# Expert slots handled in pairs, and the last token half's input projection dealt out among its attention units

## The chip, the cores and the metric

The kernel runs as one program on one core of a Trainium2 chip. The metric is the device time of one execution, in microseconds. TensorE is called PE below, VectorE DVE, ScalarE ACT, GpSimd POOL and SyncE SP.

## What is computed

Two transformer blocks follow each other on 512 tokens of width 1024, all in float32.

The first block ends with a mixture of tiny experts (PEER). For each token and each of 8 heads, 16 experts are chosen out of 16,384. Each chosen expert has a row `u` and a row `v` of 1024 numbers:

```python
pre = jnp.einsum('cd,chkd->chk', hc, u[ec])
coef = gc * jax.nn.gelu(pre, approximate=False)
out = jnp.einsum('chk,chkd->cd', coef, v[ec])
```

The second block puts 16 learned tokens ahead of the 512, normalizes, and projects to queries, keys, values (8 heads of 64), 8 forget gates and 512 pooling channels. Queries and keys are normalized per head. Then it computes

```python
s = einsum("bhqd,bhkd->bhqk", q, k) * scale + (cum_logf_q - cum_logf_k)   # causal, then softmax
p = softmax(s);  a_out = einsum("bhqk,bhkd->bhqd", p, v)
pooled[g] = trailing_mean(u[g], window 2, 4, 8 or 16) - u[g];  p_out = (pooled @ w_pool) * pool_scale
h = h + concat(a_out, p_out) @ w_out
h = h + (silu(n2 @ w_gate) * (n2 @ w_up)) @ w_down
```

The first block's attention, gates and projections come before all of this and are not touched by the change.

## The kernel before, in words

**Expert slots.** Four tiles of 128 tokens times 8 heads times 16 experts make 512 slots, numbered n. For each slot POOL issues one indirect DMA (`gather`, L1560) that fetches for 128 tokens a row of 8 KB, u and v together, about 1.05 MB. There are 8 buffers (`SLOT = 8`); a buffer is refilled when PE has used it (`rows_used`). Then DVE multiplies with the token and sums (`dots(n)`, L1585), ACT applies Gelu, multiplies with the router weight and writes a diagonal matrix (`diagonal(n)`: L1299, L1303, L1309), and PE adds the weighted v rows into PSUM (`combine(n)`, L850). `combine` is called at even n only and takes slots n and n+1 together, 8 matrix products on 64 x 64 quarters of the array. ACT and DVE handle one slot in each turn of their loops. Between the slots DVE chooses the experts of later heads (`choose`, cut into parts by `PLAN`), with one exponential on ACT (`best_weights`, L1264).

**The second block in two halves.** `block2(g)` is written once for each engine as a Python generator and works on a pair of token tiles, 256 tokens: g = 0 with the 16 learned tokens ahead (272 columns), then g = 1. The generators count ticks; `ticks.until(t)` yields until tick t, and the fixed numbers `T_IN`, `T_A`, `T_O` and so on say at which tick a step stands. For g = 0 the generators run inside the slot loops: after the work of slot n each engine advances its generator by `ticks_at(n)`, which is 0 up to slot 275 and from there 1, and 2 at every fourth slot (5 ticks in 4 slots). For g = 1 the generators run after the last slot, with nothing between the ticks. Each engine executes its own program in order; engines wait for each other by semaphores only.

**Order inside one half.** Two norms; 12 tiles of the input projection (4 of queries, 4 of keys, 4 of pooling channels; `in`, L925, 8 products each), with for each of the 8 query and key tiles a product that sums squares (`square`, L921), a logarithm and an exponential on ACT (`root`, L1334 and L1336) and a scaling on DVE; the forget gates (L931); the values (L945); the trailing means on DVE and four pooling products (L956). Only then come the 16 attention units, two per head, u = 0 to 15, one per 128 tokens. In the half g = 1 unit u works on 400 (u even) or 528 (u odd) keys:

- PE `scores(u)`: three products each, q times k with 64 rows (L972), the cumulated gates with 8 rows (L973), the causal mask (L975). 528 columns don't fit one bank, so odd units do it for 16 and for 512 columns.
- DVE takes the maximum (L1953), ACT the exponential with its sum (L1416), DVE the reciprocal (L1959), ACT scales (L1427).
- PE `transposes(u)` (L986, L988, L990), ACT copies them out of PSUM (L1440 to L1443), PE `values(u)` (L1004, L1006).
- On PE the order is scores(u), values(u-3), transposes(u-1); ACT and DVE handle unit u three ticks after PE's scores(u).

After the units come the output projection (L1028), which waits for all parts of `mix`, a norm, gate and up projections (L1046) and the down projection (L1059).

**Weights** come through SP's queue in a fixed order into a ring of 4 slots of 512 KB, each refilled when PE has finished the tile that was in it (`tile_done`). PSUM banks are handed out ahead of time by `bank_claims`, in program order.

Of the kernel before, what the change touches and what calls it, by code (L numbers as in the profile page):

```python
# [57 lines left out]
T_IN, T_FG, T_V, T_POOLED, T_P, T_A, T_O, T_U, T_D, T_END = 20, 44, 46, 47, 59, 62, 120, 146, 234, 285  # L58
ROTATE = [(0, 1, 2, 3), tuple(range(8))]
# [16 lines left out]
def ticks_at(n):  # L76

    return 0 if n < FIRST_TICK else 1 + (n % 4 == 0)

# [5 lines left out]
def bank_claims():  # L85

    table, count, sums = {}, [0] * 8, [0] * 8
    for g in range(2):
# [15 lines left out]
        for m in range(12):  # L104
            next_bank("in", m)
            if 3 <= m < 11:
                next_bank("square", m - 3)
        next_bank("forget")
        for b in range(3 - g):
            next_bank("v", b)  # L110
        for b in range(2):
            next_bank("pool", b)
# [82 lines left out]
def program(nc, xT, metaT, cond, w_ada, small, onehot, rel_bias, w_stream, sub_keys, experts, outT):  # L195
# [5 lines left out]
    with ctx:  # L201
# [116 lines left out]
        h_tok = take(TT, D)  # L318
        rows = take(SLOT, 2 * D)
# [33 lines left out]
        pooled = mix[:, 0:4, :]  # L353
# [18 lines left out]
        pool_a, pool_b = prob  # L372
# [16 lines left out]
        def wait_full(eng, g, *name):  # L389

            if name[0] in BY_TILE:
# [9 lines left out]
        def bank_of(g, *name):  # L401
            return CLAIMS[(g, *name)][0][0]
# [125 lines left out]
        def _(sp_eng):  # L528
# [35 lines left out]
            for n in range(FIRST_BLOCK // SLOTS * SLOTS, RING_TILES):  # L564
# [4 lines left out]
                eng.wait_ge(tile_done.sem, tile_done.ready(n - SLOTS))  # L569
                eng.dma_start(ring[:, n % SLOTS, :], w_stream[n if n < FIRST_BLOCK else FIRST_BLOCK + t])\  # L570
# [8 lines left out]
        def _(pe):  # L579
# [290 lines left out]
            def block2(g):  # L870
# [40 lines left out]
                for m in range(12):  # L911
# [16 lines left out]
                yield from ticks.until(T_FG)  # L928
                b = taken("forget")
                for k in range(KT):  # L930
                    last = mm(bank(b, wide)[0:NH, :], vec[:, B_FG + k * NH:B_FG + (k + 1) * NH], n_t[:, k, 0:wide],  # L931
                              start=k == 0, stop=k == KT - 1)
                last.then_inc(bank_full[b], 1)

                for t in range(4):
                    for c in range(3 - g):
# [13 lines left out]
                yield from ticks.until(T_P)  # L950
                w = stationary(B_POOL)
                for c in range(4):
                    if c % 2 == 0:
                        b = taken("pool", c // 2)
                    pe.wait_ge(pooled_ready.sem, pooled_ready.ready(g * 4 + c))
                    last = mm(bank(b, PAIR, c % 2 * PAIR), w[:, c, :], pooled[:, c, :], start=True, stop=True)  # L956
                last.then_inc(tile_done.sem, 1)

                def scores(u):
# [4 lines left out]
                    if u % 4 == 0:  # L964
                        pe.wait_ge(qk2_ready.sem, qk2_ready.ready(g * 8 + 4 + u // 4))
# [43 lines left out]
                for u in range(19):  # L1009
# [55 lines left out]
            for n in range(HEADS * PK):  # L1065
# [12 lines left out]
                for _ in range(ticks_at(n)):  # L1078
                    next(pair, None)
# [9 lines left out]
        def _(act):  # L1089
# [206 lines left out]
            def diagonal(n):  # L1296
                s = n % SLOT
                act.wait_ge(pre_done.sem, pre_done.ready(n))
                steps(op(pre[:, s:s + 1], pre[:, s:s + 1], ACT.Gelu))  # L1299
# [3 lines left out]
                steps(op(coef[:, s:s + 1], pre[:, s:s + 1], ACT.Copy, scale=wgt[:, n // P % 2, n % P:n % P + 1]))  # L1303
                if n >= SLOT:
                    act.wait_ge(rows_used.sem, rows_used.free(n, SLOT))
# [3 lines left out]
                op(diag[:, s, :], ident_pair, ACT.Copy, scale=coef[:, s:s + 1]).then_inc(diag_done.sem, 1)  # L1309
# [7 lines left out]
            def block2(g):  # L1317
# [39 lines left out]
                for m in range(12):  # L1357
                    if m < 12:
                        yield from ticks.until(T_IN + 2 * m + 4)
                        b = full("in", m)  # L1360
                        if m == 0 and g == 0:
                            act.wait_ge(chosen.sem, chosen.ready(3 * PH - 1))
                        dst = (q2[:, m % 4, 0:wide], k2[:, m % 4, cols], u2[:, m % 4, cols])[m // 4]
                        ins = op(dst, bank(b, wide), ACT.Copy)
                        ins.then_inc(in_ready.sem, 1)
                        if m < 8:
                            if m >= 3:
                                full("square", m - 3)
                            steps(op(square2[:, m % 3, 0:wide], bank(b, wide), ACT.Square))
                            steps.wait()  # L1370
                            act.sem_inc(square2_ready.sem, 1)
                        act.wait_ge(in_ready.sem, in_ready.ready(g * 12 + m))
                        act.sem_inc(bank_free[b], 1)
                    if 3 <= m < 11:
                        if m >= 5:
                            act.wait_ge(root2_used.sem, root2_used.ready(g * 8 + m - 5))
                        root((m - 3) % 2, wide, "square", m - 3)

                yield from ticks.until(T_FG + 4)
                act.wait_ge(forget_ready.sem, forget_ready.ready(g))  # L1380
                if g == 0:
                    act.preload_act_table_set("natural_log_exp_and_others")
                steps(op(logs[0:NH, 0:wide], logs[0:NH, 0:wide], ACT.Exp, scale=-1.0))
                steps.wait()
                op(logs[0:NH, 0:wide], logs[0:NH, 0:wide], ACT.Ln, bias=1.0).then_inc(forget_log.sem, 1)

                for c in range(3 - g):
                    yield from ticks.until(T_V + 12 + c)
# [10 lines left out]
                for c in range(4):  # L1399
                    yield from ticks.until(T_P + 3 + c // 2)  # L1400
# [4 lines left out]
                    else:  # L1405
# [3 lines left out]
                        act.sem_inc(bank_free[b], 1)  # L1409

# [39 lines left out]
                for u in range(19):  # L1450
# [3 lines left out]
                    if u % 4 == 2 and u > 2:  # L1454
                        b = full("y", u // 4 - 1)
                        steps(op(mix[:, u // 4 - 1, :], bank(b, PAIR), ACT.Copy))
                        steps.wait()
                        act.sem_inc(mix_ready.sem, 1)
                        act.sem_inc(bank_free[b], 1)
# [26 lines left out]
            for n in range(HEADS * PK):  # L1486
                h, c = n // PK, n % PK
                diagonal(n)
# [14 lines left out]
                for _ in range(ticks_at(n)):  # L1503
                    next(pair, None)
# [63 lines left out]
        def _(dve):  # L1568
# [296 lines left out]
            def block2(g):  # L1865
# [31 lines left out]
                for m in range(8):  # L1897
                    yield from ticks.until(T_IN + 2 * m + 12)
                    roots(2 + m)
                    dve.wait_ge(in_ready.sem, in_ready.ready(g * 12 + m))  # L1900
                    a = q2[:, m, 0:wide] if m < 4 else k2[:, m - 4, cols]
                    gain = col[:, 12:13] if m < 4 else vec[:, QN + 1:QN + 2]
                    steps(stt(a, a, gain, root2[m % 2][:, 0:wide], ALU.mult, ALU.mult))
# [4 lines left out]
                yield from ticks.until(T_FG + 3)  # L1908
                b = full("forget")
                steps(V.tensor_scalar(forget[0:NH, 0:wide], bank(b, wide)[0:NH, :], vec[0:NH, BF:BF + 1], None, ALU.add))  # L1910
                tell(dve, steps, bank_free[b])
                steps(stt(logs[0:NH, 0:wide], forget[0:NH, 0:wide], -1.0, forget[0:NH, 0:wide], ALU.mult, ALU.max))
                tell(dve, steps, forget_ready)

                n = 0
                for c in range(4):
# [4 lines left out]
                    for a in range(c + 1):  # L1921
                        yield from ticks.until(T_POOLED + n // 2)
                        n += 1
                        dst = (pool_a, pool_b)[a % 2]
# [5 lines left out]
                    yield from ticks.until(T_POOLED + n // 2)  # L1930
                    n += 1
                    steps(stt(pooled[:, c, :], src[:, META:META + PAIR], 1.0 / (2 << c), u[:, META:], ALU.mult, ALU.subtract))
                    tell(dve, steps, pooled_ready)
                    if c == 1:
                        dve.wait_ge(forget_log.sem, forget_log.ready(g))
                        steps(stt(forget[0:NH, 0:wide], forget[0:NH, 0:wide], 0.0, logs[0:NH, 0:wide], ALU.min, ALU.subtract))
                        steps.wait()
                        steps(V.tensor_tensor_scan(cum[0:NH, cols], ones[0:NH, 0:1].to_broadcast([NH, wide]),
                                                   forget[0:NH, 0:wide], 0.0, ALU.mult, ALU.add))
                        steps.wait()  # L1940
# [152 lines left out]
```

## Time and profile before

| | |
|---|---|
| median of 3 runs | 2644.8 us (2644.13 to 2647.96) |
| the profiled execution | 2649.4 us, its span 2647.6 us |
| mean granted PE clock | 0.89 |
| busy: PE, DVE, ACT, POOL | 2197.7, 1327.1, 1036.6, 581.2 us |
| expert rows by the indirect DMAs | 540.07 MB in 512 gathers |
| expert slots | from about 690 to 2166 us |
| half g = 1 of the second block | from about 2176 us to the end |

Busy time is given per engine; a PE that is busy is not PE at its full clock. The granted clock is 1.00 at 2.4 GHz and 0.50 at 1.2 GHz.

### The profile page before, as it was taken

The page shows a single profiled execution, that of the slowest core. Times are in us where ns is not written, and L with a number is a line of the kernel's source. Part 1 is how long each engine was busy: PE and PEld are TensorE (multiplying, and loading weights), DVE is VectorE, ACT ScalarE, POOL GpSimd, SP SyncE. Part 2 cuts the span into 40 slices and gives each one's busy share as a digit, 9 for nine tenths or more (in the row PEclk, how much of TensorE's full clock was granted, in tenths as well). Part 3 has the DMA queues.
Part 4 walks back from the last instruction along what each step waited for, and adds up shares of the span by engine and source line. Part 5 has one row for each costly group of instructions (what it writes and reads, how often), then busy time and mean ns, then how long its engine had stood idle before and what let it go on. Part 6 is the DMA issues. An engine that isn't in the chain of part 4 may idle for free.

```text
span 2647.6 us, 30679 instructions
## 1 busy us (share of the span) xinstructions
PE 2197.7 (83%) x10876; PEld 1328.3 (50%) x10876; DVE 1327.1 (50%) x3152; ACT 1036.6 (39%) x2580; POOL 581.2 (22%) x568
## 2 busy tenths in 40 slices
PE   5999999998777656555667876789999969999999
PEld 3877567777433112111124422356666637558888
DVE  7743744445766777777776555643334332101000
ACT  3124534423454444444446656645554232321000
POOL 0000000001343444444444223333333310000000
PEclk9999999999888777877678988899999989559999
DMA  8721011234899999999999888899999963004455
GB/s 335 271 72 48 0 40 56 64 97 146 354 420 421 419 421 413 421 413 419 415 404 397 318 325 298 309 395 409 412 411 411 418 258 119 17 0 129 153 156 151
DMA packets 124276, 710.51 MB, mean 268 GB/s; under 512 B 14648, under 2 KB 16824, under 8 KB 58464
## 3 DMA queue, kind: packets, MB, share of 16 engines
q0 software_dynamic: 74432, 540.07, 50.4%
q1 hardware_dynamic: 49456, 168.38, 18.4%
q8 instruction: 83, 1.36, 0.2%
q14 instruction: 65, 0.53, 0.1%
q10 hardware_dynamic: 240, 0.16, 0.0%
HBM read 706.45 MB, written 2.12 MB: 268 GB/s over the span
## 4 chain that ended last, share of the span: by engine, by line
PE 62%; DMA 20%; ACT 8%; DVE 5%; issue 3%; POOL 2%; ACTq 0%; SPq 0%; POOLq 0%; DVEq 0%
DMA arena<-experts,eidx 18%; PE psum L1046 11%; PE psum L850 11%; PE psum L595 5%; PE psum L596 5%; PE psum L597 5%; PE psum L1059 4%; DVE arena L1585 3%; PE psum L925 3%; PE psum L1028 2%; POOL arena L1560 2%; ACT L1299 1%; PE psum L707 1%; PE psum L973 1%; PE psum L972 1%
## 5 line engine op out<-in xcount | busy, mean ns | idle before, releaser
L850 PE MATMUL psum<-arena,sq 64*64 64x512 f32 x4096 | 640.4, 752 | 382.1 <-ACT sq L1309 360.9
L1585 DVE CUSTOM_DVE_ANT_0 arena<-arena 128x1024 f32<-128x1024 f32 x560 | 679.2, 1224 | 270.1 <-DMA arena<-experts,eidx 235.8
L1560 POOL DMA_INDIRECT arena<-experts,eidx x512 | 566.2, 1106 | 1031.6 <-PE psum L850 843.4
L850 PEld LDWEIGHTS psum<-arena,sq 64*64 64x64 f32 x4096 | 155.2, 157 | 778.4 <-ACT sq L1309 528.6
L1299 ACT ACTIVATE arena<-arena 128x1 f32<-128x1 f32 x512 | 103.0, 201 | 589.0 <-DVE arena L1585 579.7
L1046 PE MATMUL psum<-n_t,ring 128*128 128x256 f32 x1408 | 313.7, 382 | 1.7 <-DVE n_t L1582 1.7
L1046 PEld LDWEIGHTS psum<-n_t,ring 128*128 128x128 f32 x1408 | 264.5, 190 | 65.0 <-issue 30.5
L1309 ACT ACTIVATE sq<-sq,arena 128x64 f32<-128x64 f32 x512 | 178.1, 348 | 49.8 <-ACT arena L1303 2.2
L595 PE MATMUL psum<-hn_high,w_high 128*128 128x512 f32 (+1 forms) x432 | 178.9, 414 | 15.0 <-DVE hn_low L1582 13.6
L596 PE MATMUL psum<-hn_low,w_high 128*128 128x512 f32 (+1 forms) x432 | 173.5, 402 | 0.0
L597 PE MATMUL psum<-hn_high,ring_low 128*128 128x512 f32 (+1 forms) x432 | 172.3, 399 | 0.0
L1303 ACT ACTIVATE arena<-arena 128x1 f32<-128x1 f32 x512 | 150.7, 294 | 19.0
L1110 ACT ACTIVATE w_high<-ring 128x1024 fp32r<-128x1024 f32 x74 | 77.8, 1055 | 131.1 <-PE psum L597 129.3
L595 PEld LDWEIGHTS psum<-hn_high,w_high 128*128 128x128 f32 (+1 forms) x432 | 81.9, 190 | 63.0 <-issue 37.5
L1603 DVE TENSOR_TENSOR ring_low<-ring,w_high 128x1024 fp32r<-128x1024 f32 x74 | 90.1, 1219 | 40.2 <-ACT w_high L1110 38.5
L1299 ACT ACT_TABLE_LOAD x77 | 98.8, 1283 | 8.4 <-ACT hn_rest L1479 4.8
L1953 DVE TENSOR_REDUCE col<-psum 128x1 f32<-128x144 f32 (+3 forms) x32 | 16.2, 505 | 154.1 <-PE psum L975 154.1
L597 PEld LDWEIGHTS psum<-hn_high,ring_low 128*128 128x128 f32 (+1 forms) x432 | 82.1, 190 | 20.1
L925 PE MATMUL psum<-n_t,ring 128*128 128x272 f32 (+1 forms) x384 | 90.4, 388 | 1.7 <-DVE n_t L1582 1.7
L596 PEld LDWEIGHTS psum<-hn_low,w_high 128*128 128x128 f32 (+1 forms) x432 | 82.5, 191 | 17.3
L925 PEld LDWEIGHTS psum<-n_t,ring 128*128 128x128 f32 x384 | 72.2, 190 | 20.4 <-issue 8.6
L1479 ACT ACTIVATE hn_rest<-psum 128x256 f32<-128x256 f32 x44 | 16.9, 384 | 156.6 <-PE psum L1046 155.9
(271 smaller groups left out, 2810.1 us busy)
## 6 DMA issues: line engine op xcount, KB each, us to landing
ring<-w_stream SPq DMA_DIRECT2D x264, 512.0 KB
arena<-w_ada SPq DMA_DIRECT2D x48, 512.0 KB, 6.1
arena<-experts,eidx POOLq DMA_INDIRECT x512
x<-xT SPq DMA_DIRECT2D x1, 2048.0 KB, 15.0
arena<-rel_rows POOLq DMA_DIRECT2D x1, 2048.0 KB, 11.9
outT<-hn_rest SPq DMA_DIRECT2D x16, 128.0 KB
arena<-sub_keys POOLq DMA_DIRECT2D x1, 1024.0 KB, 6.4
arena<-cond SPq DMA_DIRECT2D x1, 512.0 KB, 4.2
```

The costliest lines, as they stand in the source:

```text
L595: mm(out, a[0], b[0], start=start, stop=False)
L596: mm(out, a[0], b[1], start=False, stop=False)
L597: return mm(out, a[1], b[0], start=False, stop=stop)
L850: last = mm(bank(4 + 2 * odd + a)[HALF * b:HALF * b + HALF, :], diag[k, s, :], rows[k, s, D + a * 512:D + (a + 1) * 512], start=c == 0, st ...
L925: last = mm(bank(b, wide), w[:, k, :], n_t[:, k, 0:wide], start=k == 0, stop=k == KT - 1)
L1046: last = mm(bank(b, PAIR), w[:, k, :], n_t[:, k, 0:PAIR], start=k == 0, stop=k == KT - 1)
L1059: last = mm(bank(b, PAIR), w[:, f % 8, :], act_ff[f], start=f == 0, stop=f == FF - 1)
L1299: steps(op(pre[:, s:s + 1], pre[:, s:s + 1], ACT.Gelu))
L1303: steps(op(coef[:, s:s + 1], pre[:, s:s + 1], ACT.Copy, scale=wgt[:, n // P % 2, n % P:n % P + 1]))
L1309: op(diag[:, s, :], ident_pair, ACT.Copy, scale=coef[:, s:s + 1]).then_inc(diag_done.sem, 1)
L1560: nc.gpsimd.indirect_dma_start(rows[:, s, :], None, experts, bass.IndirectOffsetOnAxis(ap=eidx[:, n // P % 2, n % P:n % P + 1], axis=0)).t ...
L1585: return V.tensor_tensor_reduce(out=out, in0=a, in1=b, scale=1.0, scalar=0.0 if op1 == ALU.add else TAKEN, op0=op0, op1=op1, accum_out=accum)
```

## The change

**Slots in pairs.** ACT and DVE handle slots n and n+1 at even n: DVE does `dots(n)` and `dots(n + 1)` one after the other, ACT one Gelu over two columns, two scalings and two diagonals. The generators of the second block advance only at odd n, by the ticks of both slots, on all three engines.

**The half g = 1.** Its weight tiles come in another order (`LAST_ORDER`): query tile 0, key tile 0, the four value tiles, then query 1, key 1, query 2, key 2, query 3, key 3, the four pooling tiles and the pooling weights. Ahead of the attention units stand only `in` 0 and 1, the gates, the values and `in` 2; the other nine `in` tiles (in halves of 4 products), six of the squares' products with their roots and scalings, and the trailing means are dealt out among units 0 to 15, and the pooling products stand behind values(15). values(u) is done one unit sooner on PE: scores(u), projection pieces, squares, transposes(u-1), values(u-2). The trailing means get buffers of their own in the space of the expert rows, and PSUM banks are claimed anew. The half g = 0 keeps its order.

```diff
+LAST_ORDER = (0, 4, 12, 13, 14, 15, 1, 5, 2, 6, 3, 7, 8, 9, 10, 11, 16)
+SQUARE_AT = {2: 0, 3: 1, 4: 2, 5: 4, 6: 5, 7: 7}
+LAST_DENSE = [(3, 0), (3, 1), (4, 0), (4, 1), (5, 0), None, (5, 1), None, (6, 0), (6, 1), (7, 0), None, (7, 1), None,
+              (8, 0), None, (8, 1), None, (9, 0), None, (9, 1), None, (10, 0), None, (10, 1), None, (11, 0), None,
+              (11, 1), None]
...
+def pair_ticks(n):
+
+    return ticks_at(n - 1) + ticks_at(n) if n % 2 else 0
...
+            for m in range(2, 12):
+                claim(("in", m), 1)
+                if m < 8:
+                    claim(("square", m), 6)
...
-                    claim(("turned_meta", u), 6)
+                    claim(("turned_meta", u), 3)
...
+                if g:
+                    yield from ticks.until(T_IN)
+                    in_product(0, range(KT))
+                    in_product(1, range(KT))
+                    forget_gates()
+                    for t in range(4):
+                        value_rows(t, 2 + t)
+                        if t in (1, 3):
+                            square_sum(t // 2)
+                    in_product(2, range(KT))
+                    for u in range(19):
+                        if u < 16:
+                            scores(u)
+                        for piece in LAST_DENSE[2 * u:2 * u + 2] if u < 15 else ():
+                            if piece:
+                                r, part_of = piece
+                                in_product(r, range(4 * part_of, 4 * part_of + 4))
+                        for r in range(2, 8):
+                            if u == SQUARE_AT[r]:
+                                square_sum(r)
+                        if 1 <= u <= 16:
+                            transposes(u - 1)
+                        if u >= 2 and u <= 17:
+                            values(u - 2)
+                        if u == 17:
+                            pool_products()
+                    yield from ticks.until(T_O)
...
-            def diagonal(n):
+            def diagonals(n):
+
                 s = n % SLOT
-                act.wait_ge(pre_done.sem, pre_done.ready(n))
-                steps(op(pre[:, s:s + 1], pre[:, s:s + 1], ACT.Gelu))
+                act.wait_ge(pre_done.sem, pre_done.ready(n + 1))
+                steps(op(pre[:, s:s + 2], pre[:, s:s + 2], ACT.Gelu))
...
+                for c in range(2):
+                    k = (n + c) % P
+                    steps(op(coef[:, s + c:s + c + 1], pre[:, s + c:s + c + 1], ACT.Copy,
+                             scale=wgt[:, n // P % 2, k:k + 1]))
                 if n >= SLOT:
-                    act.wait_ge(rows_used.sem, rows_used.free(n, SLOT))
+                    act.wait_ge(rows_used.sem, rows_used.free(n + 1, SLOT))
                 steps.wait()
...
+                for c in range(2):
+                    op(diag[:, s + c, :], ident_pair, ACT.Copy, scale=coef[:, s + c:s + c + 1]).then_inc(diag_done.sem, 1)
...
+                if g:
+                    yield from ticks.until(T_IN)
+                    take_in(0)
+                    take_in(1)
+                    forget_logs()
+                    root_of(0)
+                    root_of(1)
+                    take_values(0)
+                    take_values(1)
+                    take_in(2)
+                    for u in range(19):
+                        if u % 4 == 2 and u > 2:
+                            take_y(u // 4 - 1)
+                        if u < 16:
+                            exponents(u)
+                            normalize(u)
+                        for r in range(3, 12):
+                            if LAST_DENSE.index((r, 1)) // 2 == u:
+                                take_in(r)
+                        if 1 <= u <= 16:
+                            copy_turned(u - 1)
+                        for r in range(2, 8):
+                            if u == SQUARE_AT[r]:
+                                root_of(r)
+                    for c in range(4):
+                        take_pool(c)
+                    yield from ticks.until(T_O)
...
-                dots(n)
+                if n % 2 == 0:
+                    dots(n)
+                    dots(n + 1)
...
-                for _ in range(ticks_at(n)):
+                for _ in range(pair_ticks(n)):
                     next(pair, None)
```

DVE's part of the half g = 1 follows the same order: `forget_sums()`, `cumulate()`, `scale_in(0)`, `scale_in(1)`, then for each unit `row_top(u)`, `row_share(u)`, the scalings of `SQUARE_AT`, and one unit after the second half of a pooling tile its trailing means.

## Rows read from the trace of the kernel before

**Rows 1.** The page: busy time of each engine, its share, its instructions.

```profile
PE 2197.7 (83%) x10876; PEld 1328.3 (50%) x10876; DVE 1327.1 (50%) x3152; ACT 1036.6 (39%) x2580; POOL 581.2 (22%) x568
```

**Rows 2.** Stretches: busy PE, PEld, DVE, ACT, POOL; granted clock, DMA share, GB/s.

```profile
690.00:1390.00 700.00, 443.30 (x2537) 144.39 (x2536) 515.28 (x1387) 313.92 (x942) 300.89 (x275) 0.78 1.01 416
...
1545.00:1712.00 167.00, 113.26 (x618) 42.67 (x616) 91.51 (x276) 110.98 (x285) 58.09 (x49) 0.81 0.79 296
1712.00:2083.00 371.00, 348.75 (x1975) 227.29 (x1972) 152.06 (x276) 165.58 (x416) 122.44 (x113) 0.99 1.01 409
...
2188.40:2251.00 62.60, 62.60 (x257) 47.09 (x258) 14.85 (x34) 14.75 (x38) 0.00 (x0) 1.00 0.42 126
2251.00:2383.40 132.40, 131.79 (x369) 71.99 (x367) 12.87 (x32) 37.74 (x90) 0.00 (x0) 0.54 0.03 8
```

**Rows 3.** The same view: first block's attention, start and end of the last attention.

```profile
400.00:460.00 60.00, 60.00 (x278) 42.42 (x277) 22.17 (x62) 30.35 (x66) 0.00 (x0) 1.00 0.18 55
2251.00:2256.00 5.00, 5.00 (x21) 3.15 (x20) 0.57 (x1) 3.31 (x7) 0.00 (x0) 1.00 0.66 200
...
2380.00:2383.00 3.00, 2.74 (x20) 1.85 (x18) 0.00 (x0) 0.96 (x3) 0.00 (x0) 1.00 0.00 0
```

**Rows 4.** Groups by line from 400 to 460 us: busy, mean ns, idle before.

```profile
L595 PE MATMUL psum<-hn_high,w_high 128*128 128x512 f32 x52 | 21.8, 420 | 0.0
```

**Rows 5.** The chain that ended last, same stretch: start, share of the chain, line.

```profile
434.69 0.23 PE psum L597
```

**Rows 6.** PE's timeline in the last attention, a pair of units: start, duration, line, shapes.

```profile
2300.80 2.07 PE L972 MATMUL psum<-arena,w_rest 64*128 64x512 f32 x2
...
2305.50 0.69 PE L1004 MATMUL psum<-hn_rest,arena 16*64 16x128 f32 x2
...
2308.54 1.70 PE L972 MATMUL psum<-arena,w_rest 64*128 64x400 f32 x2
...
2312.52 0.69 PE L1004 MATMUL psum<-w_rest,arena 16*64 16x128 f32 x2
...
2316.20 0.61 PE L972 MATMUL psum<-arena,w_rest 64*128 64x16 f32 x2
```

**Rows 7.** The same timeline at both ends of that attention.

```profile
2252.62 0.94 PE L972 MATMUL psum<-arena,w_rest 64*128 64x400 f32 x2
...
2254.80 0.39 PE L972 MATMUL psum<-arena,w_rest 64*128 64x16 f32 x2
...
2255.76 1.12 PE L972 MATMUL psum<-arena,w_rest 64*128 64x512 f32 x2
...
2381.65 1.09 PE L1006 MATMUL psum<-w_rest,arena 128*64 128x128 f32 x8
```

**Rows 8.** The chain again, in the projection of g = 1.

```profile
2200.68 0.43 PE psum L921 x2
2201.11 3.45 PE psum L925 x16
...
2250.97 1.73 PE psum L956 x8
```

**Rows 9.** ACT's timeline: two of the four copies behind the pooling products.

```profile
2253.78 0.84 ACT L1402 ACTIVATE mix<-psum,vec 128x256 f32<-128x256 f32 x2 [0.21 <-ACT mix L1402]
```

**Rows 10.** PE's timeline, attention of g = 0 among the slots.

```profile
1602.01 3.48 PE L850 MATMUL psum<-arena,sq 64*64 64x512 f32 x16 [4.33 <-ACT sq L1309]
...
1612.09 3.56 PE L850 MATMUL psum<-arena,sq 64*64 64x512 f32 x16 [3.95 <-ACT sq L1309]
```

**Rows 11.** ACT's timeline between them.

```profile
1607.21 1.28 ACT L1416 ACT_TABLE_LOAD   x1 [3.61 <-DVE col L1953]
...
1609.76 1.28 ACT L1299 ACT_TABLE_LOAD   x1 [0.19 <-ACT mix L1456]
1611.06 0.20 ACT L1299 ACTIVATE arena<-arena 128x1 f32<-128x1 f32 x1
...
1611.69 0.35 ACT L1309 ACTIVATE sq<-sq,arena 128x64 f32<-128x64 f32 x1
```

More of the change, by code:

```diff
@@ L371, in program @@
         prob_t = [inside(tail_of_hn, 2 * L2, 5, P), inside(w_rest, 4 * WIDE[0], 5, P)]
-        pool_a, pool_b = prob
+        sums_of = [prob, [inside(arena, rows_at + 4 * PAIR + c * (META + PAIR), META + PAIR) for c in range(2)]]
         silu = inside(tail_of_hn, 6 * PAIR, 2, PAIR)
@@ new lines, in pool_products @@
+                def pool_products():
+                    w = stationary(B_POOL)
+                    for c in range(4):
+                        if c % 2 == 0:
+                            b = taken("pool", c // 2)
+                        pe.wait_ge(pooled_ready.sem, pooled_ready.ready(g * 4 + c))
+                        last = mm(bank(b, PAIR, c % 2 * PAIR), w[:, c, :], pooled[g][:, c, :], start=True, stop=True)
+                    last.then_inc(tile_done.sem, 1)
+                for m in range(12 if g == 0 else 0):
@@ L926, in block2 @@
                     last.then_inc(tile_done.sem, 1)
[L928 to L936, printed above, removed]
+                if g == 0:
+                    yield from ticks.until(T_FG)
+                    forget_gates()
+                for t in range(4 if g == 0 else 0):
+                    for c in range(3):
                         yield from ticks.until(T_V + 3 * t + c)
@@ L948, in block2 @@
                             last.then_inc(tile_done.sem, 1)
[L950 to L957, printed above, removed]
+                if g == 0:
+                    yield from ticks.until(T_P)
+                    pool_products()
                 def scores(u):
@@ L1355, in block2 @@
                 root(0, wide, "norm")
[L1357 to L1388, printed above, removed]
+                def take_in(r):
+                    m = IN_ORDER[g][r]
+                    b = full("in", r)
+                    if m == 0 and g == 0:
+                        act.wait_ge(chosen.sem, chosen.ready(3 * PH - 1))
+                    dst = (q2[:, m % 4, 0:wide], k2[:, m % 4, cols], u2[:, m % 4, cols])[m // 4]
+                    op(dst, bank(b, wide), ACT.Copy).then_inc(in_ready.sem, 1)
+                    if r < 8:
+                        if r >= 3:
+                            full("square", r - 3)
+                        steps(op(square2[:, r % 3, 0:wide], bank(b, wide), ACT.Square))
+                        steps.wait()
+                        act.sem_inc(square2_ready.sem, 1)
+                    act.wait_ge(in_ready.sem, in_ready.ready(g * 12 + r))
+                    act.sem_inc(bank_free[b], 1)
@@ L1397, in block2, with take_pool @@
                     act.sem_inc(bank_free[b], 1)
-                for c in range(4):
-                    yield from ticks.until(T_P + 3 + c // 2)
+                def take_pool(c):
                     b = full("pool", c // 2)
@@ L1454, in block2 @@
                     if u % 4 == 2 and u > 2:
[L1455 to L1459, printed above, removed]
+                        take_y(u // 4 - 1)
                     if u < 16:
@@ L1502, in _ @@
                     sum_out(n // P - 1)
-                for _ in range(ticks_at(n)):
+                for _ in range(pair_ticks(n)):
                     next(pair, None)
```

232 lines of the change are left out of this document (171 added, 61 removed).

## The prediction

> **What bounds the kernel now.** I read the page first: PE is busy 2197.7 of 2647.6 us, every other engine half the time or less [rows 1]. An average over stages says little, so the next view is busy time by stretch [rows 2]. Four things are to be seen there. From 690 to 1390 us the DMA share is 1.01 at 416 GB/s: the expert rows set the pace, the engines have slack. From 1545 to 1712, where the attention of g = 0 runs among the slots, the rate is 296 GB/s, and neither PE (113.26 of 167) nor ACT (110.98) nor DVE (91.51) is full: a chain between engines binds. From 1712 to 2083 PE is busy 348.75 of 371 and the DMA share is 1.01 again; both are full. From 2188.4 to the end nothing but the half g = 1 runs. Its projection holds PE for 62.6 of 62.6 us at clock 1.00, its attention for 131.79 of 132.40 us, but at 0.54. So the last attention is bound by PE at its lower level of 1.2 GHz, while ACT works 37.74 us and DVE 12.87.
>
> Next, what the clock follows. It was 1.00 when the units began, from 2251 to 2256 [rows 3], is 0.54 over the stage, and is 1.00 again at its very end, when scores no longer come and only values and transposes are left, though PE has a little idle time there, from 2380 to 2383 [rows 3]. In the first block's attention, which also has products with 64 rows, 60 us pass at 1.00 with PE full [rows 3]. There half tiles of a dense projection stand between the units: 52 products by each of three such lines [rows 4] at 0.23 us of the chain [rows 5] are 156 x 0.23 = 36 us, 60% of PE's time.
>
> **The change, part 1: the dealt-out projection.** The window is 2188.4 to 2383.4, 195.0 us.
>
> Before the units: PE loses nine `in` tiles and six squares' products: 9 x 3.45 + 6 x 0.43 = 33.6 us [rows 8]. 62.6 - 33.6 = 29.0 us remain, at full clock as before.
>
> Units at the lower level: one pair repeats every 17.0 us. 512-column scores take 2305.50 - 2300.80 = 4.70, values and transposes 3.04 and 3.68, 400-column scores 3.98, the 16-column piece 1.61 [rows 6]. Eight pairs: 136.1 us.
>
> Units at the full clock: the 400-column scores took 2.18 and the 16-column piece 0.96; the 512-column L972 took 1.12 for 2.07, so I take 0.54 of 4.70, 2.54 [rows 6, 7]. No row has a pair's values and transposes at full clock. Between no gain (6.72) and half (3.36) I take 0.55, which is what the scores did (values of an odd unit, 1.09 us for eight products, fit that) [rows 7]: 3.70. Sum 9.4, eight pairs 75.0 us.
>
> The nine tiles and six squares cost 33.6 at full clock and, with nothing else to hide it, 67.3 at the lower. So the dealt stage is 108.7 us at full clock and 203.4 at the lower; time at the lower level does 0.53 of the work. With a share h of its time low it takes 108.7/(1 - 0.47h).
>
> h decides the change. One end is the stage as it is (almost all low), the other the first block's attention (none low) [rows 2, 3]. Units 0, 1 and 4 get a whole tile, the other twelve up to 14 half a tile: 1.73 us of full-size products against 4.7 of the unit's own at full clock, 27% of PE's time, less than half of the 60% in the first block. Unit 15 gets none. The projection's products come straight behind the scores, the part with 64 and 8 rows that pulled the clock down, and the long 512-column scores of odd units (2.5 us at full clock) are the weak spots. I expect the clock to swing between its levels and take h = 0.4, mean 0.8, as in the mixed stage of g = 0 (0.81) [rows 2]: 133.6 us. Ends: h = 0 and h = 1.
>
> Who waits in the new order? A unit lasts 6 us or more on PE, ACT needs 37.74/16 = 2.4 for it [rows 2] and, for a projection tile's copy and square and a root's two steps, four passes over 256 columns at 0.42 [rows 9], 1.7 at most, so ACT and DVE stay hidden. `turned_meta` shares bank 3 with the scores of odd units: scores(u+2) waits for ACT's copy of unit u, which stands behind exponents(u+1) and take_in; PE has transposes and values(u-1) meanwhile, so about even, nothing added. Weights: 126 GB/s was enough for the projection when it ran without a break [rows 2]; dealt out it asks for less, and SP's queue keeps its one-tile-per-tile order. The trailing means (DVE) lie beside units. The end is exposed: for the last units no projection covers the way over ACT (I allow 1.8), the pooling products are now behind values(15) (1.7, moved, paid inside the 132.4 before) and their four copies on ACT delay `mix` (twice 0.84 + 0.21: 2.1) [rows 8, 9]; they were hidden. The output projection queues behind all of this, and may start at the lower clock (1.5). Together 7.1.
>
> After: 29.0 + 133.6 + 7.1 = 169.7 for 195.0, **-25 us**. Bounds: h = 0 and no slow start, 143.3 (-52); h = 1, with the pooling twice as long, 241.2 (+46).
>
> The Trainium skill ("TensorE: Matmul & The Clock Gate", Part 1, "What's actually happening") says that the gate is set by how busy PE has been recently, and that continuous work brings the full clock. The last attention contradicts it as a rule on busy time alone: 131.79 of 132.40 us busy at 0.54 [rows 2]. By that rule a reordering of equally busy work could not move the clock.
>
> **Part 2: slots in pairs.** Gelu over two columns instead of two Gelus saves one 0.20 instruction and a hop per pair; but the last slot's way over ACT, now 0.98 (1611.06 to 1611.69 + 0.35) [rows 11], gets the other slot's scaling and diagonal in it, about +0.45. Where the DMA queue is full (690 to 1390, 1712 to 2083) a refill that is asked for 0.45 us later still finds a queue, as 8 buffers are in use: 0. DVE too now waits for slot n+1's rows before it goes on to choosing; at 515.28 of 700 us [rows 2] it has room.
>
> From 1545 to 1712 the order matters. The rows show one bad round: combine at 1602.01, next at 1612.09, after 3.95 us of idle PE, itself at the low clock (3.56) [rows 10]. In between ACT sat in a table load for the exponential that had waited 3.61 us for DVE's maximum (of scores PE had issued just behind the first combine), then loaded Gelu's table (1.28), and only then handled the pair's second slot [rows 11]. So combine(n+2) waited for scores issued after combine(n), since ticks(n) stood between the two slots on ACT and DVE. In pairs, both slots come ahead of the ticks; that dependence has a whole pair more of time. The exponential's two loads per unit stay: 2 x 1.28. The 58 ticks from T_A to T_O are 46 slots, 23 pairs, at 7.2 us now. Bounds: the DMA pace of 416 GB/s would give 167 x 296/416 = 119 us (-48); a pure latency price of 0.45 x 23 gives +10. ACT's own work is 111 us, 4.8 per pair, and it must still wait for DVE twice a unit. I take 6.5 per pair, 149 us: **-18 us**. A slot done sooner is time off the end, as what follows is paid per slot; but from 1712 on both PE and DMA are full, so nothing is gained there.
>
> **Sum.** -25 - 18 = -43. The profiled execution took 2649.4 (span 2647.6), so 2606; the median of the runs is 4.6 lower, 2644.8, so I predict **2602 us**.
>
> **Rivals.**
> - *The clock is restored for good* (h near 0). For: the first block's attention at 1.00. Against: less than half its dense share. -52 - 18: 2575. Chance 0.17.
> - *The projection is dragged down* (h near 1; this one ends slower). The units' own low activity holds the clock at 1.2 GHz, and the nine tiles cost double where they now lie. For: 132 us at 0.54 with PE full. Against: dense pieces of 1.7 us and more in every unit. +46 - 18: 2673. It decides from h = 0.83, where the dealt stage takes 177 us and eats part 2's gain too. Chance 0.10.
> - *Order doesn't move the clock*: tiles at full speed, units at half, as if busy time alone counted; only the tail (about +4) is added. -14: 2631. The skill's rule named above leads here. Chance 0.05.
> - *Pairs bring nothing*: the waits in 1545 to 1712 go to DVE's wait for slot n+1 or to three ticks in a row, and ACT's table loads set the pace. For: ACT and DVE are each above half busy there. -25 alone, or -18 with part of the latency price: 2620 to 2627. Chance 0.14.
> - *Pairs hurt*: the later refill and the blocked DVE empty the DMA queue from 690 on (256 pairs at 0.1 or more), 2640 and up. Chance 0.04.
>
> Forecast: 0.50, own range 2588 to 2618. Range 2570 to 2636 leaves out the dragged-down case, the hurting pairs and the extreme of the first rival. A measurement of this kernel can tell about 0.2% from no change. Faster by more: 0.86; within: 0.03; slower: 0.11.
>
> **What would show it.** The granted clock from the first unit to the output projection, 0.75 to 0.85 (1.00, or 0.5, for the first two rivals); that stretch with the 29 us ahead at about 168; PE idle a little around the last values, and ACT's pooling copies just ahead of L1028. From the start of g = 0's attention to its output projection about 149 us, a rate of 320 to 340 GB/s, no combines 10 us apart. Slot time from 690 to 1390 unchanged. The prediction is wrong if h lies above 0.8, if scores wait for banks in the new order, or if the slot stages before 1390 lengthen.

## The result and the profile after

The changed kernel takes 2553.93 us (median of 4 runs, 2541.06 to 2563.74); the kernel before, run beside it, 2644.47 us (median of 4, 2642.2 to 2647.96). The ratio is 0.9654, with a 95% interval of 0.9609 to 0.9699. That is 91 us less, where 43 were forecast, and 16 us below the low end of the range. The profiled execution took 2555.75 us, its span 2553.8 us, 93.8 less than the span before.

The page of the changed kernel, against [rows 1]: the same number of products, 258 ACT instructions fewer.

```profile
PE 2147.7 (84%) x10876; PEld 1309.5 (51%) x10876; DVE 1340.0 (52%) x3152; ACT 932.8 (37%) x2322; POOL 592.7 (23%) x568
```

Busy time by stretch of the changed kernel (columns as in [rows 2]); the cuts are where a step starts: slot stage, the projection of g = 0 (1458.00), its attention (1539.10), its output projection (1664.30), then g = 1 with the part ahead of its units (2131.40), its units up to just ahead of the large scores of u = 15 (2160.20 to 2273.00), and the start of its output projection (2287.80).

```profile
690.00:1390.00 700.00, 438.09 (x2531) 141.90 (x2532) 521.51 (x1385) 257.19 (x802) 319.84 (x276) 0.79 1.01 417
...
1458.00:1539.10 81.10, 77.55 (x379) 36.58 (x377) 57.25 (x150) 48.98 (x112) 24.14 (x23) 1.00 0.96 364
1539.10:1664.30 125.20, 104.89 (x605) 41.01 (x601) 93.60 (x273) 98.86 (x247) 55.53 (x48) 0.86 0.98 400
1664.30:2028.00 363.70, 348.67 (x1985) 227.94 (x1982) 156.27 (x279) 143.99 (x359) 120.89 (x114) 1.00 1.02 418
...
2131.40:2160.20 28.80, 28.75 (x100) 17.15 (x100) 5.97 (x14) 5.01 (x12) 0.00 (x0) 1.00 0.34 110
2160.20:2273.00 112.80, 112.70 (x473) 74.52 (x473) 18.52 (x45) 41.89 (x104) 0.00 (x0) 0.88 0.15 45
...
2287.80:2292.00 4.20, 4.15 (x12) 3.40 (x13) 0.00 (x0) 0.00 (x0) 0.00 (x0) 0.60 0.19 75
```

The same view of the kernel before, cut at the same steps:

```profile
1457.00:1549.70 92.70, 79.27 (x378) 36.65 (x376) 56.68 (x152) 55.05 (x125) 22.66 (x22) 0.98 0.87 331
1549.70:1712.50 162.80, 111.51 (x604) 42.15 (x600) 91.13 (x273) 107.26 (x272) 57.17 (x48) 0.81 0.79 295
1712.50:2083.00 370.50, 348.25 (x1975) 227.29 (x1972) 151.97 (x276) 165.42 (x415) 122.44 (x113) 0.99 1.01 409
```

To be seen: up to the projection of g = 0 the two kernels go alike (the changed one is there 1.0 us later; 690 to 1390 moves 417 GB/s for 416 [rows 2]). Then 92.7 us become 81.1, the attention's 162.8 become 125.2, and the next 370.5 become 363.7. The rest up to the last combine gives 2.8 more. Together the last combine ends at 2108.5 for 2166.2: 57.8 us sooner, which the experiments below put down to the slots in pairs. In the attention the DMA share is 0.98 for 0.79 and the rate 400 GB/s for 295. It now runs close to the 417 GB/s of the slot stage, where the expert rows set the pace, but not quite at it.

The two ends of the stretch that follows, in the chain that ended last (start, duration, what ran), of the kernel before:

```profile
2162.48 3.76 PE psum L850 x16
...
2383.35 27.86 PE psum L1028 x128
```

and of the changed kernel:

```profile
2106.46 2.02 PE psum L882 x16
...
2287.85 29.55 PE psum L1120 x128
```

From the end of the last combine to the output projection of g = 1 it is 179.4 us for 217.1, 37.7 less, from the dealt-out projection. That output projection starts at a lower clock (0.60 in its first 4.2 us), and 1.7 us go back there (29.55 for 27.86); all behind it is equal. The sum: -57.8 - 37.7 + 1.7 = -93.8.

### The profile page after: what moved, and what is told of

Same layout as the page of the kernel before. It is cut to its first block, busy times and chain, and to the rows that moved or that the text cites. A ratio compares the mean times of both kernels' runs of the same rounds, so it can differ in the third digit from the quotient of the medians.

```text
span 2553.8 us, 30169 instructions
## 1 busy us (share of the span) xinstructions
PE 2147.7 (84%) x10876; PEld 1309.5 (51%) x10876; DVE 1340.0 (52%) x3152; ACT 932.8 (37%) x2322; POOL 592.7 (23%) x568
## 4 chain that ended last, share of the span: by engine, by line
PE 57%; DMA 27%; DVE 6%; ACT 5%; issue 3%; POOL 2%; SPq 0%; ACTq 0%; POOLq 0%; DVEq 0%
DMA arena<-experts,eidx 26%; PE psum L1138 9%; PE psum L882 9%; PE psum L627 6%; PE psum L628 5%; PE psum L629 5%; DVE arena L1725 3%; PE psum L1151 3%; POOL arena L1700 2%; PE psum L1120 2%; PE psum L949 2%; PE psum L999 2%; PE psum L739 1%; ACT sq L1406 1%; PE psum L715 1%
## 5 line engine op out<-in xcount | busy, mean ns | idle before, releaser
L882 PE MATMUL psum<-arena,sq 64*64 64x512 f32 x4096 | 626.4, 737 | 333.6 <-ACT sq L1406 326.4
L1700 POOL DMA_INDIRECT arena<-experts,eidx x512 | 577.8, 1128 | 963.8 <-PE psum L882 771.9
L1392 ACT ACTIVATE arena<-arena 128x2 f32<-128x2 f32 x256 | 52.0, 203 | 722.1 <-DVE arena L1725 720.7
L1138 PEld LDWEIGHTS psum<-n_t,ring 128*128 128x128 f32 x1408 | 264.3, 190 | 66.1 <-issue 30.5
L1406 ACT ACTIVATE sq<-sq,arena 128x64 f32<-128x64 f32 x512 | 150.3, 340 | 24.9 <-ACT arena L1398 1.5
L1398 ACT ACTIVATE arena<-arena 128x1 f32<-128x1 f32 x512 | 122.9, 287 | 10.4
L1689 POOL TENSOR_SCALAR_AFFINE_SELECT arena<-arena 128x128 f32<-128x128 f32 x32 | 9.3, 292 | 271.9 <-DVE arena L1722 271.5
L1120 PE MATMUL psum<-mix,ring 128*128 128x256 f32 x256 | 59.0, 390 | 2.1 <-ACTq L1502 2.1
L1151 PE MATMUL psum<-w_rest,ring 128*128 128x256 f32 x256 | 59.0, 381 | 0.0
```

The source lines that it names most:

```text
L882: last = mm(bank(4 + 2 * odd + a)[HALF * b:HALF * b + HALF, :], diag[k, s, :], rows[k, s, D + a * 512:D + (a + 1) * 512], start=c == 0, st ...
L1120: last = mm(bank(b, PAIR), w[:, k, :], mix[:, k, :], start=k == 0, stop=k == KT - 1)
L1138: last = mm(bank(b, PAIR), w[:, k, :], n_t[:, k, 0:PAIR], start=k == 0, stop=k == KT - 1)
L1151: last = mm(bank(b, PAIR), w[:, f % 8, :], act_ff[f], start=f == 0, stop=f == FF - 1)
L1392: steps(op(pre[:, s:s + 2], pre[:, s:s + 2], ACT.Gelu))
L1398: steps(op(coef[:, s + c:s + c + 1], pre[:, s + c:s + c + 1], ACT.Copy, scale=wgt[:, n // P % 2, k:k + 1]))
```

## Where the attention of g = 0 lost its wait

Waits of PE and ACT in that stretch, of the kernel before (who waited for whom: us in total, times, longest us):

```profile
PE psum L850 <- ACT sq L1309: 53.6, 19, 4.7
...
ACT L1416 <- DVE col L1953: 26.1, 6, 5.8
```

and of the changed kernel:

```profile
PE psum L882 <- ACT sq L1406: 17.1, 15, 3.0
...
ACT L1525 <- DVE col L2089: 2.7, 4, 1.8
```

ACT's wait for DVE's maximum (L2089), ahead of each exponential, is all but gone, and with it two thirds of PE's wait for the diagonals. PE's timeline in a stretch of the changed kernel that answers to [rows 10] shows combines 6.2 and 8.7 us apart with no idle time ahead of the later two. In the whole attention of g = 0 none lie further apart than these 8.7 us, where six pairs of neighbours lay 9.6 to 11.8 us apart before:

```profile
1593.60 3.69 PE L882 MATMUL psum<-arena,sq 64*64 64x512 f32 x16 [1.54 <-ACT sq L1406]
...
1602.32 3.69 PE L882 MATMUL psum<-arena,sq 64*64 64x512 f32 x16
...
1608.49 1.95 PE L882 MATMUL psum<-arena,sq 64*64 64x512 f32 x16
```

ACT's timeline between them, against [rows 11]: exponential and Gelu each still load their table, 1.28 us, but a Gelu now serves two slots (`arena 128x2`), and both diagonals follow in one go.

```profile
1603.76 1.28 ACT L1392 ACT_TABLE_LOAD   x1 [0.17 <-ACT hn_rest L1525]
1605.05 0.20 ACT L1392 ACTIVATE arena<-arena 128x2 f32<-128x2 f32 x1
...
1605.87 0.66 ACT L1406 ACTIVATE sq<-sq,arena 128x64 f32<-128x64 f32 x2
```

## The experiments

**The parts alone.** First each half of the change by itself, in the kernel before: the slots in pairs, and the half g = 1 as dealt out.

> The kernel before with the slots in pairs and nothing else; the half g = 1 keeps its old order. If the two parts are independent and the slot stage lost 57.7 us by the pairs (last combine's end 2166.2 before, 2108.5 after), this gives 2644 - 58 = 2587 us, and the last attention stays at 132 us and clock 0.54. If part of the gain came from the dealt-out projection instead (other banks, other weights order), less: down to 2626 for the 18 us that the prediction gave the pairs.

Measured: 2592.8 us (2590.0 to 2598.22), ratio 0.9801 (0.9774 to 0.9829): 52 us. The attention of g = 0 takes 124.6 us, the last combine ends at 2112.3, and the last attention is as it was: 130.7 us to its output projection.

> The changed kernel with one slot at a time on ACT and DVE and the ticks after each slot, as before; the half g = 1 has its new order. Independent parts: 2644 - 37 = 2607 us, last combine as before at about 2166, projection and units 156 us. If the clock of the units depends on where in time they start, it varies by several us between executions, as the four runs of the changed kernel do (2541 to 2564).

Measured: 2605.18 us (2599.17 to 2612.0), ratio 0.9844 (0.9812 to 0.9877): 40 us. Its slots end at 2165.8 for 2166.2 and the attention of g = 0 takes 160.1 for 162.8. The units' stretch, to the last values, is 122.0 us at a mean clock of 0.87. 52 and 40 make 92, where the whole change gave 91: within the spread of the runs the parts add up, and neither needs the other.

**What in the pairs does it.** The order alone: both slots ahead of the ticks on all engines, but with ACT's old instructions, one Gelu per slot.

```diff
-                diagonal(n)
+                if n % 2 == 0:
+                    diagonal(n)
+                    diagonal(n + 1)
...
-                for _ in range(ticks_at(n)):
+                for _ in range(pair_ticks(n)):
...
-                dots(n)
+                if n % 2 == 0:
+                    dots(n)
+                    dots(n + 1)
```

> Pairs alone as in the first run, but ACT keeps its single instructions: Gelu, scaling, diagonal for slot n, then for n+1, both ahead of the ticks; DVE too does both dots ahead of the ticks. Theory of order (a combine no longer waits for scores that PE issued right behind the combine before): nearly all of the gain stays, 2587 to 2592 us. Theory of instructions (ACT is short of time among its table loads, and 256 Gelus fewer free it): most of it goes, 2625 or more.

The instructions alone: ACT's new `diagonals` for two slots, but at the odd slot, behind the even slot's ticks; DVE and all ticks as before.

```diff
-                diagonal(n)
+                if n % 2:
+                    diagonals(n - 1)
```

> The kernel before with ACT's paired instructions (one Gelu for two slots), but done at odd n, behind the even slot's ticks, with the ticks after each slot as before; DVE as before. Theory of order: the even slot's ticks still stand ahead of the pair's last work on ACT, so 2635 to 2655 us, no gain. Theory of instructions: about 2587 to 2600.

And the order on PE and DVE only, as in the first diff without ACT's part:

> The kernel before with DVE alone taking both dots ahead of both slots' ticks; ACT takes slot n, ticks(n), slot n+1, ticks(n+1) as before. If the wait that costs is on ACT (the exponential of a unit and its table load between the pair's two slots), little is gained, 2635 to 2648 us. If it is on DVE (the maximum and the reciprocal ahead of the second dot), about 2590 to 2600.

Measured: the order alone 2587.94 us (2583.78 to 2594.33), ratio 0.9788 (0.9759 to 0.9818), all of the gain. The instructions alone 2655.74, ratio 1.0036 (1.0021 to 1.0051), a small loss. The order on PE and DVE, called "on DVE alone" from here, 2634.42, ratio 0.9967 (0.995 to 0.9984), 9 us. The last combine of the order alone ends at 2108.3, as in the changed kernel. The stretch of g = 0's attention in the order alone:

```profile
1533.60:1663.60 130.00, 107.25 (x604) 41.79 (x600) 93.00 (x275) 107.49 (x276) 53.17 (x48) 0.84 0.97 383
```

The same stretch takes 161.8 us at 300 GB/s in the instructions alone and 159.0 at 302 in the order on DVE alone. ACT's wait for the maximum in it, in the order alone:

```profile
ACT L1421 <- DVE col L1960: 1.2, 2, 0.9
```

in the instructions alone:

```profile
ACT L1421 <- DVE col L1959: 31.6, 8, 6.4
```

in the order on DVE alone:

```profile
ACT L1421 <- DVE col L1958: 22.7, 6, 4.3
```

In the order alone ACT is busy 107.49 us, as much as before (107.26), and still the stretch runs at a DMA share of 0.97: ACT's work was not what bound it. The two that keep ACT's second slot behind the first one's ticks keep the wait for the maximum (31.6 and 22.7 us) and the 300 GB/s. It is the order on ACT and DVE together that pays. The saved instructions add nothing that can be seen in the whole time: with them the stretch takes 124.6 us for 130.0, but the last combine ends 4 us later (2112.3 for 2108.3). The counterpart, the order on PE and ACT without DVE, has no time: ACT's and DVE's programs then wait for each other in a circle. ACT would want DVE's second dot before it goes on, DVE's second dot would stand behind its ticks, and these want ACT's exponential. So no run shows what ACT's order would give by itself.

One profile is not the whole story here. The last attention is the same program in the kernel before, the pairs alone, the order alone, the instructions alone and the order on DVE alone. It took 130.7 us from its first scores to the output projection in three of their profiled executions, but 121.4 at a clock of 0.58 in the order alone and 124.5 at 0.56 in the instructions alone. What sets off these brief returns to the full clock, no run shows. Of the 9.9 us by which the profiled execution of the order alone is shorter than that of the pairs alone, 9.3 lie there.

**What the clock follows.** To part "dense columns lift the clock" from "PE is busy enough already", the kernel before was given more work, whose result nothing reads: four extra products in each unit of the last attention, right behind `scores(u)`, identity by 256 token columns. In one run they have 128 rows, in the other 8. "Dense" here means products that stream through all 128 rows.

```diff
+                def filler():
+                    if g:
+                        for k in range(4):
+                            mm(bank(1, PAIR), ident[0:128, :], n_t[0:128, k, 0:PAIR], start=True, stop=True)
...
                         scores(u)
+                        filler()
```

> The kernel before with four more products in each unit of the last attention, behind its scores: the identity (128 rows) times 256 columns of n_t into bank 1, which nobody reads. It is 64 products more, 27.7 us at full clock (55 at the lower), and nothing is taken away. Theory of the clock (what the products stream decides it): the clock of the stage rises from 0.54 to 0.8 to 0.95, and 132 us become 75 + 28 divided by (1 - 0.47h), h = 0.1 to 0.4: 108 to 127, so the kernel gets faster by 5 to 24 us with more work. Rival (the dealt-out order gains by hiding ACT's and DVE's steps, or by anything else than the clock): slower by 28 to 55 us.

> The same 64 products with 8 rows instead of 128, so PE is as busy as in the run with 128 rows. If busy time decides the clock, this run is like that one. If it is what the products stream (rows), the clock stays at about 0.5 and the stage grows by some 55 us, to about 2700.

Measured: with 128 rows 2626.92 us, ratio 0.9939 (0.9919 to 0.9958): more work, and faster. With 8 rows 2708.99, ratio 1.0237 (1.022 to 1.0254). The stretch from the first scores to the output projection, with 128 rows:

```profile
2251.00:2360.60 109.60, 108.99 (x489) 69.58 (x489) 12.88 (x32) 35.77 (x86) 0.00 (x0) 0.94 0.02 6
```

with 8 rows:

```profile
2254.70:2442.50 187.80, 187.22 (x488) 109.32 (x488) 12.87 (x32) 36.03 (x86) 0.00 (x0) 0.53 0.01 3
```

One unit's filler in PE's timeline, with 128 rows and then with 8:

```profile
2310.06 1.91 PE L982 MATMUL psum<-n_t,ident 128*128 128x256 f32 x8
```

```profile
2309.69 3.78 PE L982 MATMUL psum<-n_t,ident 8*128 8x256 f32 x8
```

Both keep PE busy for more than 99% of the stretch, as it was before [rows 2]. 16 x 1.9 = 30 us of full-height filler make the stage 21 us shorter (109.6 for 130.7, 2252.62 to 2383.35 in the kernel before), at 0.94; that is below the 121.4 to 130.7 us that the stage took without filler. 16 x 3.8 = 60 us of filler with 8 rows make it 57 longer, at 0.53. In these runs, what is streamed through few rows doesn't lift the clock, and what is streamed through all does.

The Trainium skill ("TensorE: Matmul & The Clock Gate", Part 1, "What's actually happening") sets the gate by how busy PE has been. Both runs and [rows 2] disagree with that as a rule on busy time: three stages busy beyond 99%, at 0.54, 0.94 and 0.53.

**Can the rest be had?** The changed kernel was run again beside three variants of it.

> The changed kernel once more, on the chip of the next three, so that they can be compared with it: 2554 us, spread over some 20 us, as the clock swings in the last attention.

Measured: 2550.85 us (2542.75 to 2557.07, 6 runs), ratio 0.9646 (0.9624 to 0.9668).

In the changed kernel the clock fell in seven of the eight odd units (not in u = 3): five times in the 8-row product of the 512-column scores, twice (u = 5 and 13) only in the projection piece right behind them. PE's timeline at u = 7, a fall (2.02 for 1.12, the piece of the projection behind it 3.65) and the unit after it back at 2.4 GHz (1.89):

```profile
2212.41 1.12 PE L1037 MATMUL psum<-arena,w_rest 64*128 64x512 f32 x2
2213.47 2.02 PE L1038 MATMUL psum<-arena 8*128 8x512 f32 x2
2215.41 0.77 PE L1040 MATMUL psum<-causal,ident 128*128 128x112 f32 x2
2215.97 3.65 PE L949 MATMUL psum<-n_t,ring 128*128 128x256 f32 x8
...
2224.29 1.89 PE L949 MATMUL psum<-n_t,ring 128*128 128x256 f32 x8
...
2283.76 1.99 PE L982 MATMUL psum<-arena,ring 128*128 128x256 f32 x8
2287.85 12.50 PE L1120 MATMUL psum<-mix,ring 128*128 128x256 f32 x49 [2.10 <-ACTq L1502]
```

So one variant puts the unit's first projection piece between q times k and the gates' product, to break the long run with few rows:

```diff
+                        if at == 0:
+                            for piece in between:
+                                in_product(piece[0], range(4 * piece[1], 4 * piece[1] + 4))
...
-                            scores(u)
+                            scores(u, pieces[:1])
```

> The changed kernel with one edit: the first projection piece of a unit stands between q*k and the gates' product of the unit's large scores, instead of behind the scores. Theory of the clock: the stretch in which only 64-row and 8-row products stream, where the trace shows each fall (in the 512-column scores of odd units), is cut in two, so falls get rare: clock of the units 0.95 or more for 0.88, and 108.7 us instead of 122: 10 to 14 us faster, about 2542, with less spread between executions. Rival (the place of the piece within a unit doesn't matter, only how much dense work a unit has): no change, 2554.

Measured: 2563.6 us (2555.53 to 2565.46), ratio 0.9682 (0.9662 to 0.9703), slower than the changed kernel. The expectation missed. Its stretch from the first unit to the output projection:

```profile
2156.20:2299.20 143.00, 131.68 (x526) 83.21 (x525) 21.46 (x52) 45.86 (x116) 0.00 (x0) 0.86 0.13 39
```

and the wait that it brought PE:

```profile
PE psum L1037 <- ACT w_rest L1551: 8.3, 6, 1.9
```

The next scores now wait for bank 3, that is for ACT's copy of the turned meta tokens: the piece that used to follow the scores had covered ACT's way to it. The other 7 us of the 143.0 for 127.5 in the run beside it lie mostly in PE's own time, at a clock that is no higher (0.86). The new waits also spoil the test. In the split's profiled execution the clock stayed up in the two odd units (u = 1 and 5) ahead of which PE did not wait, and fell in each of the six that came behind a wait of 0.5 to 1.9 us. So the run shows that this edit doesn't pay; whether breaking the long run with few rows would keep the clock up without the waits stays open.

The second variant moves the pooling products ahead of the transposes of unit 15, ACT's four copies with them, and the last trailing means one unit earlier:

> The changed kernel with the pooling products ahead of transposes(15), their copies ahead of the last copy of y, and the last trailing mean one unit sooner. The end of the attention (2283.76 to 2287.85: 1.99 of pooling products, 2.1 of copies) should go from the path: 3 to 4 us faster, about 2550, if the last means are ready in time; if not, PE waits for them and nothing is gained.

Measured: 2548.76 us (2548.02 to 2553.2), ratio 0.9641 (0.9622 to 0.9659), against 0.9646 for the changed kernel beside it. In its profiled execution the stage is 121.6 us for 127.5. ACT's copies of the pooling are now partly covered, and what is left of the wait ahead of the output projection is 1.07 for 2.10. The other 4.9 us are PE's own busy time, 120.4 for 125.3 at a clock of 0.90 for 0.87, and no run shows that the move is what lifted it:

```profile
2278.57 1.99 PE L982 MATMUL psum<-arena,ring 128*128 128x256 f32 x8
...
2284.71 2.61 PE L1120 MATMUL psum<-mix,ring 128*128 128x256 f32 x11 [1.07 <-ACTq L1563]
```

It has the lowest median of all kernels run, but 2 us are less than the executions of one kernel differ here, so it is not shown to beat the changed one. The last variant takes the split, the early pooling and the single ACT instructions together:

> Both edits together, and ACT with single instructions in pair order (as in the third run). The sum is 10 to 14 plus 3 to 4 us, 2536 to 2541; single instructions on ACT cost nothing or gain up to 5, if handing over the first diagonal sooner matters.

Measured: 2559.87 us (2557.09 to 2571.79), ratio 0.9692 (0.9669 to 0.9716). Its PE waits 8.4 us, 6 times, for the same copy as in the split. The sum that was expected, 2536 to 2541, missed with the split's.

## Why the prediction was wrong, step by step

- **The direction and both mechanisms** held. Dense work between the units lifted the clock (fillers, dealt alone), and the price of the slots lay in the ticks between a pair's two slots (order alone). Too small were the sizes of both, the pairs' above all.
- **The failed step is "I take 6.5 per pair, 149 us: -18 us".** Measured: 125.2 us for 23 pairs, 5.4 per pair, -37.6 in this stretch and -57.8 in all. The sum had named the bound that the measurement came near (400 GB/s of its 416), "the DMA pace of 416 GB/s would give 167 x 296/416 = 119 us (-48)", and passed it by for ACT's 4.8 us of work per pair and its waits for DVE. The order alone shows both reasons false: as much ACT work, 130.0 us; and the waits for DVE's maximum, which I took as given, were themselves made by the order (26.1 us before, 1.2 with it).
- **Two stretches beside it were priced at nothing.** The projection of g = 0 has the same ticks between two slots: 92.7 to 81.1 us, 331 to 364 GB/s, and PE's wait for the diagonals there went from 13.4 to 3.5. And "from 1712 on both PE and DMA are full, so nothing is gained there" missed 6.8 + 2.8 us: the rate went from 409 to 418 GB/s. No run shows the cause of this small part.
- **The dealt stage**: 29.0 us ahead of the units measured 28.9. The formula 108.7/(1 - 0.47h) was right, h was off. From the first scores to the last values (2160.33 to 2283.76) the mean clock is 0.86, a share of 0.28 at the lower level. That gives 125.2 us; measured are 123.4. With 0.4 I had 133.6. The guesses at the full clock held too: a pair's values and transposes took 3.71 us there, for the 3.70 assumed. So the term that was mis-sized is h, borrowed from a stage with another mix, the attention of g = 0 among the slots. That the other mix is why it was too high is my reading, not shown; the rows gave no share for this mix.
- **The tail**: 7.1 us allowed, 5.8 measured: pooling 1.99, wait 2.10, later 1.7 at the lower clock. The 1.8 for the last units' way over ACT didn't show.
- **What was costed at nothing and was nothing**: the slot stage before 1390, the weights, the banks. For bank 3 the result was right and the reason incomplete. The prediction named the transposes and values(u-1) as the cover for ACT's copy. With these in place and the projection piece moved away, 8.3 us of wait appear (split): the piece behind the scores is a needed part of the cover.
- **Rivals.** Restored for good, dragged down, clock unmoved by order: none; the clock lay between the first and the forecast. Pairs bring nothing, or hurt: no; there was no rival in which the pairs reach the DMA's pace, though the bound was worked out. With it (-48) and the measured h (29.0 + 125.2 + 7.1 = 161.3 for 195.0, -33.7) the sum would have been 2644.8 - 48 - 33.7 = 2563 us.

## What to carry to other kernels

When an engine program takes turns between two streams of work, look for what the partner of a pair waits for across the other stream: group the pair on every engine in the chain, since here grouping on PE and DVE alone left the wait. If such a chain is broken, price the stretch by the next resource that fills up (here the DMA rate of the neighbouring stretches), not by the busy time of the engine that was seen waiting, and apply it to every stretch with the same pattern. If PE is fully busy at 1.2 GHz in a stage of products with few rows, put dense products of another stage among them, even a few, and check which wait they cover before moving them again.

## What the runs showed of the hardware

- PE without idle time stayed at 1.2 GHz for nearly all of 130.7 us (mean clock 0.53) while many of its products streamed 8 or 64 rows. 30 us of added products with 128 rows make the stage 21 us shorter, at 0.94.
- How much of such a stage runs at 1.2 GHz differs between executions of the same instructions: the unchanged last attention took 130.7 us in three profiled executions, 124.5 and 121.4 in two others. So a single profile can't tell apart two variants whose difference is below some 10 us there.
- The changed kernel's executions lay 23 us apart in the first comparison (4 runs) and 14 us in the last (6 runs); those of the kernel before beside them 6 us (4 runs) and 14 us (11 runs). The runs don't show that the change makes the time less steady.
